# A decoder step on one core: where sixteen groups of cached values stand between the matmuls of the last head

## The chip, the cores and the metric

The kernel runs on one core of a Trainium2 chip. Its time is the device time of one execution in microseconds (us), as the median of several. Five engines work side by side, each through its own list of instructions in order: TensorE (PE, matmuls), VectorE (DVE), ScalarE (ACT), GpSimd (POOL) and SyncE (SP, which here only issues DMAs). They wait for one another through semaphores.

## The reference, cut to what matters

One step of a one-layer decoder: a retention branch of 4 heads and an attention branch of 8 heads ("FoX") are merged and followed by a gated convolution network. Beside a prompt of 1024 tokens there are 8 samples, each with one new token and 4096 cached rows of keys and values, in 32 pages of 128 rows that a page table picks:

```python
k_past = cache_k[l][page_table].reshape(bs, past, FOX_HEADS, FOX_HD)
v_past = cache_v[l][page_table].reshape(bs, past, FOX_HEADS, FOX_HD)
...
# fox_sample
s = jnp.concatenate([jnp.einsum('bqhd,bkhd->bhqk', q, k_past), jnp.einsum('bqhd,bkhd->bhqk', q, k)], axis=-1) * scale
p = jax.nn.softmax(logits, axis=-1)          # logits: s + bias, masked
return (jnp.einsum('bhqk,bkhd->bqhd', p[..., :p_len], v_past)
        + jnp.einsum('bhqk,bkhd->bqhd', p[..., p_len:], v))
```

The change concerns the first of the two products in the last line, for the seventh sample.

## The kernel before, in words

The kernel has four stages; the third one, `retain`, computes the retention branch head by head and does the cached attention of the 8 samples between the matmuls of the heads: two samples for each of the four heads. In head h, PE multiplies the cached values of sample 2h ("values a") and DVE computes the key scores of sample 2h+1 ("keys a") at the same time; after that PE does the values of sample 2h+1 ("values b"), and DVE the keys of the next sample ("keys b", not in the last head).

**Groups.** A sample's 32 pages are 16 groups of two pages (GRP, NG). One group of values is 16 small matmuls on PE (line 948, two pages x four column blocks, each in two passes), all added up in bank 7, which no other matmul of the head uses. One group of keys is a multiply and a reduction on DVE (lines 1245 and 1249, two DVE instructions on 128x1024 elements).

**Loads.** SP issues all loads of keys and values in one list: key group, value group, key group, value group, and so on, two DMAs of 256 KB for each (line 836). Keys and values have rings of 4 buffers each (SLOTS). Before it issues value group i, SP waits until PE has done group i-4 (semaphore `v_used`), and before key group i until DVE has reduced group i-4 (`k_used`). SP runs in a loop of four pairs and reads eight pages' numbers of keys and of values at the head of each round (line 828). While value groups of the seventh sample (sample index 6) are loaded, the keys beside them are those of the eighth.

**Places.** How many groups stand at each place of PE's list is set by a tuple of 22 numbers, VALUES_A_LAST for the last head; KEYS_A_LAST does it for DVE. The sum must be 16. The first six numbers are the places after each of the three chunks of the products w4 and w5 (the retention values, `product`, 24 matmuls a chunk). The next nine are the places in the transpose loop (`rows_t`, lines 1016 and 1018), where parts of the product w6 stand between. The last seven are the places in the retention loop: for each of 8 blocks of 128 tokens PE computes scores and a state update (lines 1043 and 1044), then nine matmuls of w7 (line 142), then, with `out(t-1)`, the block's output before (lines 1032 and 1034), and then the groups. `out(t)` waits for `inner_t` of block t, which DVE makes (line 1362). After block 6, `cache_tail` (lines 955 and 959) closes the sum of the seventh sample.

**DVE's list around it.** DVE does the key groups of the transpose loop, then splits the weights w8 (line 108, `split_lo`, after ACT's `split_hi`, line 101), and only then makes `inner_t` of block 0.

**POOL's list around it.** After ACT has written the last row of the transpose loop (`rows_out`), POOL stores eight rows (line 917) and loads the weights w9, 512 KB (line 93, `load(h, 9)`). The weights w6, w7 and w8 were loaded before.

Of the kernel before, what the change touches and what calls it, by code (L numbers as in the profile page):

```python
# [705 lines left out]
PARTS = NCH * KD  # L706
VALUES_A = (0, 0, 1, 1, 1, 1) + (0, 1, 0, 1, 0, 1, 0, 1, 0) + (1, 0, 1, 1, 0, 1, 1) + (1, 0, 1, 1)
KEYS_A = (1, 1, 1, 1, 1, 1) + (0, 1, 0, 1, 0, 1, 0, 1, 0) + (1, 0, 1, 0, 1, 0, 1) + (2,)
VALUES_A_LAST = (0, 1, 2, 2, 2, 1) + (0, 1, 1, 0, 1, 1, 0, 1, 1) + (1, 0, 1, 0, 0, 0, 0)
KEYS_A_LAST = (1, 2, 1, 1, 2, 1) + (0, 1, 1, 0, 1, 1, 0, 1, 1) + (1, 0, 1, 0, 0, 0, 0)  # L710


# [3 lines left out]
KEYS_B = (4, 2) + (1, 1, 1) + (5,) + (1, 1, 0)  # L716
assert all(sum(s) == NG for s in (VALUES_A, KEYS_A, VALUES_A_LAST, KEYS_A_LAST, VALUES_B, VALUES_B_LAST, KEYS_B))


def take(counts, e):  # L720

    return range(sum(counts[:e]), sum(counts[:e + 1]))
# [7 lines left out]
def retain(nc, g, a, c, o):  # L730
# [4 lines left out]
    with ExitStack() as ctx:  # L735
# [202 lines left out]
        def on_tensor(pe):  # L938
            def cache_values(n, u, i, first):

                slot = i % SLOTS
                if first:
                    pe.wait_ge(prob, n + 1)
                    pe.wait_ge(fos_out, n)
                pe.wait_ge(v_land[slot], n * (NG // SLOTS * GRP * 16) + (i // SLOTS + 1) * GRP * 16)
                for p in range(GRP):
                    for j in range(4):
                        mm = pe.matmul(bank[7][32 * j:32 * j + 2, 0:P], score[u][:, i * GRP + p, 2 * j:2 * j + 2],  # L948
                                       vals[slot][:, p, j * P:(j + 1) * P], start=(first and p == 0), stop=False)
                mm.then_inc(v_used, 1)  # L950
# [22 lines left out]
            def body(h, last):  # L973
                def values_a(e):
                    for i in take(VALUES_A_LAST if last else VALUES_A, e):
                        cache_values(h * 2, 0, i, i == 0)
# [1242 lines left out]
```

## Time and profile before

| | |
|---|---|
| time, median of 3 runs | 2079.36 us (2076.39 to 2080.16) |
| the profiled execution | 2078.71 us, of it span 2076.8 us |
| PE busy | 1964.2 us (95% of the span) |
| DVE busy | 1143.8 us (55%) |
| ACT, POOL busy | 646.4 us (31%), 195.4 us (9%) |
| share of PE in the chain that ended last | 74% |
| mean granted clock of PE | 0.981 |

The last head runs from about 889 to 1016 us of the span. The granted clock is a share of TensorE's full speed of 2.4 GHz; 0.5 is its lower level, 1.2 GHz. A row of the timeline gives the start, the duration, the engine, the line, the operation, its output and inputs, the number of merged instructions, and in brackets the idle time ahead of it with what ended it.

### The profile page before, as it was taken

What the parts mean: (1) busy time and instruction counts of PE and PEld (TensorE: products, weight loads), DVE (VectorE), ACT (ScalarE), POOL (GpSimd) and SP (SyncE); (2) the same over time, 40 slices, a digit from 0 to 9 for tenths busy, and PEclk for the clock granted to TensorE, in tenths of its full rate; (3) what the DMA queues carried; (4) which work ended last, traced back from release to release, by engine and by line L of the source; (5) the groups of instructions that cost most, each with busy time, mean ns of one, the idle gap of its engine ahead of it and who ended that gap; (6) DMA issues with size and microseconds to landing.
All of it is one profiled execution on the core that took longest, in us unless ns stands there. A gap on an engine that the chain in (4) does not pass through costs nothing.

```text
span 2076.8 us, 38216 instructions
## 1 busy us (share of the span) xinstructions
PE 1964.2 (95%) x14259; PEld 1839.1 (89%) x14259; DVE 1143.8 (55%) x1748; ACT 646.4 (31%) x1196; POOL 195.4 (9%) x230
## 2 busy tenths in 40 slices
PE   7999999899999999979899998999999999999996
PEld 5888888788898898868799997999999999999996
DVE  5545646968867866875423857633322333234348
ACT  5445433134134133313401304433202231133334
POOL 1000000111020020010000100000000001000005
PEclk9999999999999999999999999999999999999999
DMA  5111113697987988886833411111111111211154
GB/s 155 43 42 42 41 54 104 216 323 238 323 278 245 314 273 285 285 296 226 283 92 97 119 51 31 32 51 41 51 50 41 51 40 45 58 41 41 38 163 135
DMA packets 151730, 276.63 MB, mean 133 GB/s; under 512 B 19057, under 2 KB 57982, under 8 KB 151590
## 3 DMA queue, kind: packets, MB, share of 16 engines
q1 hardware_dynamic: 115954, 175.22, 25.4%
q0 software_dynamic: 23296, 82.96, 13.7%
q10 hardware_dynamic: 12368, 16.88, 2.2%
q8 instruction: 79, 1.29, 0.3%
q14 instruction: 33, 0.27, 0.0%
HBM read 247.37 MB, written 27.72 MB: 132 GB/s over the span
## 4 chain that ended last, share of the span: by engine, by line
PE 74%; DVE 12%; DMA 4%; issue 4%; SPq 3%; ACT 2%; POOL 0%; ACTq 0%; DVEq 0%; POOLq 0%
PE bank L125 55%; PE bank L142 5%; PE bank L1718 3%; PE bank L521 2%; PE bank L948 2%; DVE cache_keys L1245 2%; PE bank L533 2%; DVE score L1249 2%; SPq L836 2%; DMA cache_keys<-in_cache_k_dram 1%; SPq L828 1%; DMA cache_vals<-in_cache_v_dram 1%; PE banks L505 1%; PE banks L507 1%; DVE w_lo L108 1%
## 5 line engine op out<-in xcount | busy, mean ns | idle before, releaser
L125 PE MATMUL bank<-x_hi,w_hi 128*128 128x344 f32 x1872 | 612.0, 327 | 16.1 <-DVE rot_sin L1315 12.6
L125 PE MATMUL bank<-x_hi,w_lo 128*128 128x344 f32 x1872 | 602.8, 322 | 0.0
L125 PE MATMUL bank<-x_lo,w_hi 128*128 128x344 f32 x1872 | 602.5, 322 | 0.0
L125 PEld LDWEIGHTS bank<-x_hi,w_hi 128*128 128x128 f32 x1872 | 356.3, 190 | 30.0 <-issue 17.4
L125 PEld LDWEIGHTS bank<-x_hi,w_lo 128*128 128x128 f32 x1872 | 356.3, 190 | 0.0
L125 PEld LDWEIGHTS bank<-x_lo,w_hi 128*128 128x128 f32 x1872 | 355.9, 190 | 0.2 <-issue 0.2
L101 ACT ACTIVATE w_hi<-w_raw 128x1024 fp32r<-128x1024 f32 (+3 forms) x139 | 142.1, 1023 | 388.9 <-PE bank L125 371.3
L125 PE MATMUL bank<-moving_lo,w_hi 128*128 128x344 f32 x744 | 239.0, 321 | 0.0
L125 PE MATMUL bank<-moving_hi,w_hi 128*128 128x344 f32 x744 | 226.0, 325 | 9.2 <-DVE moving_lo L1886 3.3
L108 DVE TENSOR_TENSOR w_lo<-w_raw,w_hi 128x1024 fp32r<-128x1024 f32 (+1 forms) x138 | 164.2, 1190 | 87.4 <-ACT w_hi L101 86.8
L125 PE MATMUL bank<-moving_hi,w_lo 128*128 128x344 f32 x648 | 209.0, 323 | 0.0
L1245 DVE TENSOR_TENSOR cache_keys<-cache_keys,q_wide 128x1024 f32<-128x1024 f32 x128 | 156.3, 1223 | 52.3 <-DMA cache_keys<-in_cache_k_dram 52.1
L1249 DVE TENSOR_REDUCE score<-cache_keys 128x16 f32<-128x1024 f32 x128 | 155.1, 1213 | 0.0
L125 PEld LDWEIGHTS bank<-moving_hi,w_hi 128*128 128x128 f32 x744 | 138.6, 191 | 12.7 <-DVE moving_lo L1886 4.6
L125 PEld LDWEIGHTS bank<-moving_lo,w_hi 128*128 128x128 f32 x744 | 141.1, 190 | 0.1
L142 PE MATMUL bank<-x_hi,w_hi 128*128 128x344 f32 x384 | 138.0, 359 | 2.3 <-DVE rv_rows L1419 2.3
L2017 DVE SCALAR_TENSOR_TENSOR stage<-stage,conv_cols_tile 128x1024 f32<-128x1024 f32 x22 | 28.3, 1284 | 185.7 <-ACT stage L1820 185.7
L125 PEld LDWEIGHTS bank<-moving_hi,w_lo 128*128 128x128 f32 x648 | 123.5, 191 | 0.0
L142 PE MATMUL bank<-x_hi,w_lo 128*128 128x344 f32 x384 | 123.0, 320 | 0.0
L142 PE MATMUL bank<-x_lo,w_hi 128*128 128x344 f32 x384 | 122.6, 319 | 0.0
L948 PE MATMUL bank<-cache_vals,score 128*2 128x128 f32 x2048 | 77.8, 274 | 24.0 <-DMA cache_vals<-in_cache_v_dram 19.8
L93 POOL DMA_DIRECT2D w_raw<-in_w_in_dram x53 | 49.0, 925 | 533.6 <-DVE w_lo L108 468.5
(292 smaller groups left out, 2817.8 us busy)
## 6 DMA issues: line engine op xcount, KB each, us to landing
cache_keys<-in_cache_k_dram SPq DMA_DIRECT2D x256, 256.0 KB, 4.9
cache_vals<-in_cache_v_dram SPq DMA_DIRECT2D x256, 256.0 KB, 5.3
w_raw<-in_w_in_dram POOLq DMA_DIRECT2D x52, 512.0 KB, 6.4
w_raw<-in_w_up_dram POOLq DMA_DIRECT2D x22, 512.0 KB, 4.6
w_raw<-in_w_gate_dram POOLq DMA_DIRECT2D x22, 512.0 KB, 4.6
tail_raw<-in_w_down_dram SPq DMA_DIRECT2D x22, 448.0 KB, 3.6
gate<-gate_t_scratch SPq DMA_DIRECT2D x15, 516.0 KB, 3.5
w_raw<-in_w_down_dram POOLq DMA_DIRECT2D x10, 448.0 KB, 4.4
```

The costliest lines, as they stand in the source:

```text
L93: eng.dma_start(g.w_raw[slot][:, 0:kt, 0:m], src).then_inc(g.w_land[slot], 16)
L101: act.activation(g.w_hi[slot][:, 0:kt, 0:m], g.w_raw[slot][:, 0:kt, 0:m], ACT.Copy).then_inc(g.w_rounded, 1)
L108: dve.tensor_tensor(g.w_lo[slot][:, 0:kt, 0:m], g.w_raw[slot][:, 0:kt, 0:m], g.w_hi[slot][:, 0:kt, 0:m].bitcast(F32), ALU.subtract).then_i ...
L125: mm = pe.matmul(g.bank[n][0:m, 0:TC], w[slot][:, k, 0:m], x[:, k, chunk(n)], start=(k == 0 and i == 0), stop=(k == kt - 1 and i == 2))
L142: mm = pe.matmul(g.bank[n][0:m, 0:TC], w[slot][:, k, 0:m], x[:, k, chunk(n)], start=(k == 0 and q == 0), stop=(k == kt - 1 and q == 2))
L521: mm = pe.transpose(bank[part][:, n * P:(n + 1) * P], prob[s % 2][:, blk * P:(blk + 1) * P], g.ident[:])
L533: pe.matmul(b[own(r), 0:P], kv[u][:, blk, 1, own(r)], prob_t[(2 * i + r) % 4][:, blk, :], start=(blk == 0), stop=(blk == i))
L836: sp.dma_start(ring[slot][:, p, :], page).then_inc(land[slot], 16)
L948: mm = pe.matmul(bank[7][32 * j:32 * j + 2, 0:P], score[u][:, i * GRP + p, 2 * j:2 * j + 2], vals[slot][:, p, j * P:(j + 1) * P], start=(f ...
L1245: dve.tensor_tensor(keys[slot][:], keys[slot][:], qb[u][:].unsqueeze(1).to_broadcast([P, GRP, FH * HD]), ALU.mult).then_inc(k_mult, 1)
L1249: dve.tensor_reduce(score[u][:, (i - 1) * GRP:i * GRP, :], keys[slot][:].rearrange("p g (h e) -> p g h e", e=HD), AX.X, ALU.add).then_inc( ...
L1718: mm = pe.matmul(bank[i % NCH][:, 0:hi - lo], w[slot][:, k, :], x[:, k, lo:hi], start=(k == 0 and q == 0), stop=(k == KT - 1 and q == 2))
```

## The change

The tuple of the last head is changed at seven places. The first stage of six places holds 0, 1, 1, 1, 1, 1 groups (five) where it held 0, 1, 2, 2, 2, 1 (eight). The second stage, of nine places, has the same numbers and six groups, but they are the groups 5 to 10 where they were 8 to 13. The third stage holds 1, 1, 1, 1, 1, 0, 0 (five) where it held 1, 0, 1, 0, 0, 0, 0 (two).

```diff
-VALUES_A_LAST = (0, 1, 2, 2, 2, 1) + (0, 1, 1, 0, 1, 1, 0, 1, 1) + (1, 0, 1, 0, 0, 0, 0)
+VALUES_A_LAST = (0, 1, 1, 1, 1, 1) + (0, 1, 1, 0, 1, 1, 0, 1, 1) + (1, 1, 1, 1, 1, 0, 0)
```

The lists of DVE, ACT, POOL and SP are unchanged, and no matmul is added or dropped on PE. The numbers behind `cache_vals` below are the ring's buffers; a group is one row of eight matmuls here (each is two passes in the trace).

PE, in product w5 of the last head, between its first chunk (bank 0) and its second (bank 1), before:

```order
L125 MATMUL bank0<-x_hi,w_hi1 128x344
L125 MATMUL bank0<-x_lo,w_hi1 128x344
L125 MATMUL bank0<-x_hi,w_lo1 128x344
L948 MATMUL bank7<-cache_vals3,score0 2x128 x8
L948 MATMUL bank7<-cache_vals0,score0 2x128 x8
L125 MATMUL bank1<-x_hi,w_hi1 128x344
```

The same place now:

```order
L125 MATMUL bank0<-x_lo,w_hi1 128x344
L125 MATMUL bank0<-x_hi,w_lo1 128x344
L948 MATMUL bank7<-cache_vals2,score0 2x128 x8
L125 MATMUL bank1<-x_hi,w_hi1 128x344
L125 MATMUL bank1<-x_lo,w_hi1 128x344
L125 MATMUL bank1<-x_hi,w_lo1 128x344
```

Two groups (3 and 4) stood here, and now one (group 2): the first reuse of a buffer, `cache_vals0`, has moved to a later place.

PE, in the retention loop, from the last w7 matmuls ahead of `out(0)` to those of block 2, before:

```order
L142 MATMUL bank1<-x_lo,w_hi1 128x344
L142 MATMUL bank1<-x_hi,w_lo1 128x344
L1032 MATMUL banks34<-rv_rows,inner_t 128x256
L1043 MATMUL banks34<-rq_t,rk_t 128x128
L1044 MATMUL banks34<-rv_rows,rk_rows 128x256
L142 MATMUL bank1<-x_hi,w_hi1 128x344
```

The same place now:

```order
L142 MATMUL bank1<-x_lo,w_hi1 128x344
L142 MATMUL bank1<-x_hi,w_lo1 128x344
L1032 MATMUL banks34<-rv_rows,inner_t 128x256
L948 MATMUL bank7<-cache_vals0,score0 2x128 x8
L1043 MATMUL banks34<-rq_t,rk_t 128x128
L1044 MATMUL banks34<-rv_rows,rk_rows 128x256
L142 MATMUL bank1<-x_hi,w_hi1 128x344
```

Group 12 (in buffer 0) now stands behind `out(0)`; before, it stood in the transpose loop. Groups 13, 14 and 15 follow behind `out(1)`, `out(2)` and `out(3)`.

## Rows read from the trace of the kernel before

**Rows 1.** The page: the chain that ended last, shares of the span by engine.

```profile
PE 74%; DVE 12%; DMA 4%; issue 4%; SPq 3%; ACT 2%; POOL 0%; ACTq 0%; DVEq 0%; POOLq 0%
```

**Rows 2.** Waits, 898 to 978 us: who waited for whom, total, times, longest.

```profile
DVE cache_keys L1245 <- DMA cache_keys<-in_cache_k_dram: 11.7, 9, 2.7
...
PE bank L948 <- DMA cache_vals<-in_cache_v_dram: 6.7, 4, 2.6
```

**Rows 3.** Timeline of PE: value groups up to the transpose loop's end.

```profile
902.09 0.62 PE L948 MATMUL bank<-cache_vals,score 128*2 128x128 f32 x16 [3.12 <-issue]
...
908.14 1.05 PE L948 MATMUL bank<-cache_vals,score 128*2 128x128 f32 x32
...
913.10 0.62 PE L948 MATMUL bank<-cache_vals,score 128*2 128x128 f32 x16
914.75 0.62 PE L948 MATMUL bank<-cache_vals,score 128*2 128x128 f32 x16 [1.04 <-DMA cache_vals<-in_cache_v_dram]
...
920.92 0.62 PE L948 MATMUL bank<-cache_vals,score 128*2 128x128 f32 x16 [1.03 <-DMA cache_vals<-in_cache_v_dram]
...
931.88 0.62 PE L948 MATMUL bank<-cache_vals,score 128*2 128x128 f32 x16 [2.62 <-DMA cache_vals<-in_cache_v_dram]
...
946.69 0.62 PE L948 MATMUL bank<-cache_vals,score 128*2 128x128 f32 x16 [2.02 <-DMA cache_vals<-in_cache_v_dram]
```

**Rows 4.** Timeline of PE: retention loop, its first block, `out(0)` and the tail.

```profile
952.63 0.38 PE L1043 MATMUL banks<-rq_t,rk_t 128*128 128x128 f32 x2
...
957.52 0.59 PE L1032 MATMUL banks<-rv_rows,inner_t 128*128 128x256 f32 x2
...
973.45 0.40 PE L955 MATMUL bank<-v_new,score 8*2 8x128 f32 x8
```

**Rows 5.** Timeline of PE: the same place one head earlier.

```profile
777.08 0.42 PE L142 MATMUL bank<-x_hi,w_hi 128*128 128x344 f32 x1
...
780.23 0.38 PE L1043 MATMUL banks<-rq_t,rk_t 128*128 128x128 f32 x2
```

**Rows 6.** Timeline of SP: value group 7, key groups 8 and 13.

```profile
917.60 0.85 SPq L836 DMA_DIRECT2D cache_vals<-in_cache_v_dram  x2
924.57 0.86 SPq L836 DMA_DIRECT2D cache_keys<-in_cache_k_dram  x2
...
942.13 0.85 SPq L836 DMA_DIRECT2D cache_keys<-in_cache_k_dram  x2
```

**Rows 7.** Timeline of DVE: key group 13, weights w8, `inner_t` of block 0.

```profile
948.14 1.23 DVE L1245 TENSOR_TENSOR cache_keys<-cache_keys,q_wide 128x1024 f32<-128x1024 f32 x1 [2.36 <-DMA cache_keys<-in_cache_k_dram]
949.29 1.21 DVE L1249 TENSOR_REDUCE score<-cache_keys 128x16 f32<-128x1024 f32 x1
952.33 1.22 DVE L108 TENSOR_TENSOR w_lo<-w_raw,w_hi 128x1024 fp32r<-128x1024 f32 x1 [1.83 <-ACT w_hi L101]
953.59 0.29 DVE L1362 TENSOR_TENSOR inner_t<-banks,head_const 128x128 f32<-128x128 f32 x1
```

**Rows 8.** Timeline of POOL: store of eight rows, load of the weights w9.

```profile
951.01 0.59 POOL L917 DMA_DIRECT2D own_values_scratch<-rv_rows  x1 [30.65 <-ACT rv_rows L1170]
952.00 0.93 POOL L93 DMA_DIRECT2D w_raw<-in_w_in_dram  x1 [0.40 <-issue]
```

**Rows 9.** Stretches: busy us of each engine; granted clock, DMA share, GB/s stand last.

```profile
889.00:895.00 6.00, 6.00 (x38) 5.95 (x34) 5.85 (x11) 0.00 (x0) 0.00 (x0) 0.64 0.68 230
...
902.00:908.00 6.00, 5.91 (x40) 5.63 (x40) 5.98 (x6) 0.00 (x0) 1.76 (x2) 0.72 1.03 302
...
948.00:952.00 4.00, 4.00 (x29) 2.85 (x29) 2.36 (x2) 1.48 (x3) 0.59 (x2) 0.58 1.04 381
```

**Rows 10.** Timeline of PE: waits ahead of the first stretch of rows 9.

```profile
884.80 0.62 PE L948 MATMUL bank<-cache_vals,score 128*2 128x128 f32 x16 [2.18 <-DMA cache_vals<-in_cache_v_dram]
887.48 1.03 PE L948 MATMUL bank<-cache_vals,score 128*2 128x128 f32 x16 [2.06 <-DMA cache_vals<-in_cache_v_dram]
```

**Rows 11.** The tile of keys, whole kernel: DMA from issue to landing.

```profile
DMA to landing us min/median/max: 2.6/4.9/10.1
```

## The prediction

> **What bounds the kernel now.** I read the page first: the chain that ended last is PE for 74% of it [rows 1]. So whatever PE waits for in the last head is time, as long as nothing else becomes later. Then I read the waits of the stretch in which the values of the seventh sample are multiplied. PE waited 6.7 us in four waits for value groups to land; beside it DVE waited 11.7 us for key groups [rows 2]. The timeline of PE shows which four: 1.04 us at group 4, 1.03 us at group 6, 2.62 us at group 8 and 2.02 us at group 12 [rows 3]. A fifth wait, 3.12 us at group 0, names no DMA [rows 3]; by the code it is for DVE's copy of the sixth sample's output, and group 0 stays at its place, so it stays too. The last thing to read is the other engines at these places, since they decide how much of 6.7 us can come back: SP [rows 6], DVE [rows 7], POOL [rows 8], and the granted clock [rows 9].
>
> **What PE's list gives by itself.** I follow PE from 908.14 us, with every delta against the profiled execution.
> - After the third chunk of w4 there is one group less. Two groups in a row took 908.14 to 909.13 us, a group alone takes about 0.55 us (a row of 0.62 us whose end overlaps the next start), so 0.44 us goes.
> - After the first chunk of w5: groups 3 and 4 began at 913.10 us, and group 4 at 914.75 us behind its wait of 1.04 us [rows 3]. Now group 2 alone stands there: 1.65 us goes, in sum 2.09.
> - After the second chunk the same with groups 5 and 6 and 1.03 us: 1.65 us, in sum 3.74.
> - In the transpose loop the waits of 2.62 and 2.02 us stood ahead of groups 8 and 12. These places now hold groups 5 and 9. Group 5 was used in the first stage before, without any wait of its own, and group 9 is issued right behind group 8 in SP's list, while PE asks for it only at the place of group 12; the four waits of rows 2 are all there were, so group 9 was landed when PE asked for it before. In sum 8.38.
> - The granted clock fell to 0.58 in 948 to 952 us, right behind the 2.02 us wait [rows 9]. From 947.24 us (the end of group 12) to the retention loop at 952.63 us [rows 4] PE took 5.39 us for the rest of w6 and w7, two transposes and one group. One head earlier the same stretch without the group took 777.08 to 780.23 us, 3.15 us [rows 5], and with a group 3.70 us. The low clock cost 1.69 us there. Without the wait it goes: in sum 10.07.
>
> So PE would come to the retention loop at 942.56 us instead of 952.63, and to `out(0)` at 957.52 - 10.07 = 947.45 us [rows 4]. In the loop it has three groups more before the tail (13, 14, 15 and 12 where it had only 15, besides the one at the first place): 3 x 0.55 = 1.65 us. If nothing else were late, the gain would be 10.07 - 1.65 = 8.4 us.
>
> **What is late next.** `out(0)` needs `inner_t` of block 0. DVE makes it behind key group 13 and the weights w8, in that order. Key group 13 is issued at 942.13 us [rows 6] and DVE, which had waited 2.36 us for it, started on it at 948.14 us [rows 7]. This time hangs on SP, not on PE: SP issued the last two rounds of loads back to back, and its last waits in the stretch were before 917.60 us. The change moves that point a little: value group 7 needs value group 3 used, which was at 913.7 us and is now at the fifth place, 919.27 - 2.09 = 917.2 us plus 0.62 us. I put the issue of value group 7 at 918.0 instead of 917.60 us, and since the reading of page numbers (918.45 to 924.57 us [rows 6]) and the issues follow without a gap, everything behind is 0.4 us later: key group 13 at 948.54 us.
> From there DVE needs the multiply (1.15), the reduction (to 950.50 before), the split of w8 (1.26) and `inner_t` (0.29). The 1.83 us that it waited for ACT's half of w8 [rows 7] go, since ACT follows PE, which is 10 us earlier. `inner_t` ends at 953.88 - 1.83 + 0.4 = 952.45 us. PE, at `out(0)` from 947.45 us on, stands for 5.0 us: one wait in place of four. `out(0)` starts 957.52 - 952.5 = 5.0 us earlier than before, and with the three groups the tail comes 5.0 - 1.65 = 3.35 us earlier. Behind that point I find no second bound: blocks 1 to 3 want `inner_t` 2.5 us or more apart, and with one key group each DVE makes them as fast; the groups of the eighth sample stand behind the tail, and the four buffers of the ring are free by 965 us.
>
> **What comes off the 3.35 us.** Two things, neither shown by the trace at this place.
> - The clock. Behind a stand of PE it falls: mean granted 0.58 over 4 us behind 2.02 us of idle, 0.72 over 6 us behind 3.12 us, 0.64 over 6 us behind 2.18 and 2.06 us [rows 3, 9, 10]. Lost are 0.42 x 4 = 1.7, 0.28 x 6 = 1.7 and 0.36 x 6 = 2.2 us. But 2.62 us at 931.88 lost nothing. A stand of 5 us costs between 0 and 2.2 us here; I take 1.5, since part of the low stretch may lie in the stand itself.
> - The load of w9. POOL issues it 1.9 us after the last row of the transpose loop, at 952.00 us [rows 8]. That row comes 9 to 10 us earlier now, so 512 KB more stand in the middle of the last round of key and value loads, where the DMA engines have a share of 1.03 to 1.04 already [rows 9]. At 381 GB/s they take 1.4 us. Key group 13 is then up to 1.4 us later, and so is `inner_t`. Bounds 0 and 1.4 us; I take half, 0.7.
> The Trainium skill, DMA: Bandwidth & Descriptors, "Issuing engines are not separate DMA queues", says that transfers of all issuing engines run on the same 16 DMA engines and interleave. By that rule the w9 load comes off in full (1.4 us) rather than by half; no row here shows such a load among key group 13's packets.
> Sum: 3.35 - 1.5 - 0.7 = 1.15 us faster. The ends are 3.35 (nothing comes off) and 3.35 - 2.2 - 1.4 = -0.25. Against the profiled execution's own 2078.71 us this gives 2077.6. That execution was 0.65 us below the median of the three runs, 2079.36; I forecast 2078.0 us, between.
>
> **The rivals.**
> - *No stand at `out(0)`.* Key group 13 would have to land before PE needs it, about 5 us earlier. Then the whole 8.4 us comes back: 2078.71 - 8.4 = 2070.3. Against it: SP issues without gaps and DVE had waited for this group before. For it only that DMA landings vary.
> - *The stand, but at full clock and without the collision.* 3.35 us faster: 2075.4. For it: 2.62 us of idle at 931.88 left the clock at 1.00.
> - *The keys come much later (slower).* The landing of a key group took 6.0 us for group 13 and up to 10.1 us elsewhere [rows 7, 11]. If w9 and the value groups push group 13 to such a landing, 4.1 us, and the clock costs 2.2, the sum is 3.35 - 4.1 - 2.2 = -2.95: 2081.7. It turns slower once group 13 lands more than about 1.9 us late at 1.5 us of clock. Against it: such landings are rare, the median is 4.9 [rows 11].
> - *The clock as the whole story.* The Trainium skill, TensorE: Matmul & The Clock Gate, "HAM oscillation — how this bites in real kernels", says that a DMA wait of PE that is long enough makes the matmuls behind it start at half clock; one long stand is then worse than several short ones. The trace agrees in part: two of the four short waits had no loss. Worked out from rows as a mechanism of this kernel, it is the stand of 5 to 6.4 us with two losses of the size of rows 9, 1.7 + 1.7, and the collision: 3.35 - 1.4 - 3.4 = -1.45, 2080.2.
>
> **Chances.** The forecast (a stand, a gain between -0.25 and 2.5 us) 0.58; full clock and no collision 0.14; no stand 0.09; two clock losses 0.09; keys much later 0.10. About 0.2%, 4.2 us, is what a measurement of this kernel tells from no change. Faster by more than that: the case without a stand, 0.09, and 0.05 for the good case with a median that falls low, so 0.14. Slower by more: half of the slower rival and a little of the clock's, 0.07. The rest, 0.79, is no change. The range that leaves out the case without a stand and the worst of the slower one is 2074.0 to 2081.5.
>
> **What would show it.** In the trace after: no wait of L948 for values at the first three chunk places, in the transpose loop none or under 1 us; L1043 of block 0 near 942.6 us; a new wait of PE at L1032 for `inner_t`, near 5 us; key group 13 on DVE at 948.5 to 950 us; w9 issued near 942.5 us; the tail L955 at 970 to 973.5 us; a low clock somewhere in 950 to 958 us. Wrong would be: value waits that stay in the transpose loop, a key group 13 that lands before 945 or after 951 us, or a difference that arises behind 979 us.

## The result and the profile after

The changed kernel takes 2081.47 us (median of 20 runs) where the kernel before takes 2077.64 us (20 runs): a ratio of 1.0021, 95% interval 1.0011 to 1.0031 (the two medians alone give 1.0018). It is slower, by 2.3 to 6.4 us; the forecast was 1.2 us faster, 2078.0 us. The measured time lies at the very end of the stated range of 2074.0 to 2081.5 us. A later series gave 1.0017 (1.0004 to 1.0030). The profiled execution has a span of 2083.6 us, 6.8 us more than before, but 2.0 us of that are there already at value group 0 of the last head, ahead of the first changed instruction, and 2.7 us arise behind the tail of the eighth sample. The prediction had called a difference behind 979 us a sign of being wrong, but these two parts can't be put down to the change: a second execution of the changed kernel (e7 below) is 6.3 us shorter ahead of value group 0 and 3.7 us shorter behind the eighth sample, and differs by less than 0.1 us in between. So I count places from the start of value group 0 of the seventh sample, which all kernels have at the same place in PE's list.

The page's chain by engine of the changed kernel, which answers to [rows 1]:

```profile
PE 75%; DVE 11%; DMA 5%; issue 4%; SPq 3%; ACT 2%; POOL 0%; ACTq 0%; DVEq 0%; POOLq 0%
```

PE and DMA have a point more, DVE a point less. The waits from 900 to 982 us answer to [rows 2]:

```profile
DVE cache_keys L1245 <- DMA cache_keys<-in_cache_k_dram: 15.9, 10, 4.7
...
PE banks L1032 <- DVE inner_t L1362: 6.7, 1, 6.7
PE bank L948 <- issue: 3.4, 1, 3.4
```

The four waits for values are gone. In their place is one of the same length, of `out(0)` for `inner_t`. The timeline of PE in the changed kernel, for [rows 3] and [rows 4]:

```profile
904.12 0.62 PE L948 MATMUL bank<-cache_vals,score 128*2 128x128 f32 x16 [3.45 <-issue]
...
944.42 0.38 PE L1043 MATMUL banks<-rq_t,rk_t 128*128 128x128 f32 x2
...
956.17 1.22 PE L1032 MATMUL banks<-rv_rows,inner_t 128*128 128x256 f32 x2 [6.69 <-DVE inner_t L1362]
...
977.41 0.40 PE L955 MATMUL bank<-v_new,score 8*2 8x128 f32 x8
```

Counted from group 0, the loop begins at 40.3 us (50.5 before), `out(0)` at 52.1 (55.4), and the tail comes at 73.3 (71.4). Of the gain of 10.2 us at the loop's start 3.4 us are left at `out(0)`, and at the tail the changed kernel is 1.9 us behind. DVE, SP and POOL, for [rows 7], [rows 6] and [rows 8]:

```profile
952.31 1.23 DVE L1245 TENSOR_TENSOR cache_keys<-cache_keys,q_wide 128x1024 f32<-128x1024 f32 x1 [2.69 <-DMA cache_keys<-in_cache_k_dram]
953.45 1.21 DVE L1249 TENSOR_REDUCE score<-cache_keys 128x16 f32<-128x1024 f32 x1
954.58 1.22 DVE L108 TENSOR_TENSOR w_lo<-w_raw,w_hi 128x1024 fp32r<-128x1024 f32 x1
955.83 0.29 DVE L1362 TENSOR_TENSOR inner_t<-banks,head_const 128x128 f32<-128x128 f32 x1
```

```profile
919.99 0.85 SPq L836 DMA_DIRECT2D cache_vals<-in_cache_v_dram  x2
926.95 0.86 SPq L836 DMA_DIRECT2D cache_keys<-in_cache_k_dram  x2
...
944.49 2.03 SPq L836 DMA_DIRECT2D cache_keys<-in_cache_k_dram  x2
```

```profile
943.40 0.59 POOL L917 DMA_DIRECT2D own_values_scratch<-rv_rows  x1 [19.80 <-ACT rv_rows L1170]
944.39 0.93 POOL L93 DMA_DIRECT2D w_raw<-in_w_in_dram  x1 [0.40 <-issue]
```

DVE does the four steps without a gap from key group 13 on, so `out(0)` is as late as that load. And the w9 load is issued in the same 0.1 us as key group 13. The clock, for [rows 9]:

```profile
952.00:956.00 4.00, 0.00 (x0) 0.00 (x0) 3.66 (x4) 0.00 (x0) 0.00 (x0) 0.55 1.06 393
956.00:960.00 4.00, 3.83 (x23) 2.45 (x24) 3.32 (x7) 0.78 (x2) 0.00 (x0) 0.50 0.48 146
960.00:964.00 4.00, 4.00 (x30) 3.36 (x29) 2.92 (x4) 0.46 (x2) 0.00 (x0) 0.67 0.30 112
```

It stands at the lower level, 1.2 GHz, for nearly all of the last 4 us of the stand (mean 0.55) and for six more behind it. The chain of waits around `out(0)` says the same in one view, the start, the length, and what the time went to:

```profile
944.49 1.51 SPq L836
946.19 6.09 DMA cache_keys<-in_cache_k_dram
952.37 1.08 issue
953.45 1.21 DVE score L1249
954.66 1.13 DVE w_lo L108
956.17 1.22 PE banks L1032 x2
```

In the kernel before, the chain at this place ran from SP over a load of values straight to PE:

```profile
939.93 0.34 SPq L836
941.55 5.10 DMA cache_vals<-in_cache_v_dram
946.69 0.62 PE bank L948 x16
```

### The profile page after: what moved, and what is told of

The parts are those of the page before. It is cut to its first block, busy times and chain, and to the rows that moved or that the text cites. A ratio compares the mean times of both kernels' runs of the same rounds, so it can differ in the third digit from the quotient of the medians.

```text
span 2083.6 us, 38216 instructions
## 1 busy us (share of the span) xinstructions
PE 1973.0 (95%) x14259; PEld 1844.5 (89%) x14259; DVE 1143.4 (55%) x1748; ACT 646.8 (31%) x1196; POOL 195.4 (9%) x230
## 4 chain that ended last, share of the span: by engine, by line
PE 75%; DVE 11%; DMA 5%; issue 4%; SPq 3%; ACT 2%; POOL 0%; ACTq 0%; DVEq 0%; POOLq 0%
PE bank L125 55%; PE bank L142 5%; PE bank L1718 3%; PE bank L948 2%; PE bank L521 2%; PE bank L533 2%; DMA cache_keys<-in_cache_k_dram 2%; DVE score L1249 2%; DVE cache_keys L1245 1%; SPq L836 1%; DMA cache_vals<-in_cache_v_dram 1%; SPq L828 1%; PE banks L505 1%; PE banks L507 1%; DVE w_lo L108 1%
```

## The experiments

Theory K: the change lets PE run ahead until it meets `inner_t` of block 0, which hangs on the load of key group 13; the clock that falls behind this one stand, and dearer places of the groups, turn the gain into a loss. Rival G: the loss is the price of the groups in the retention loop. Rival M: keys only move a wait. All ratios are to the kernel before on the same chip, with 95% intervals, from 12 runs each (e5: 6, the first series of the changed kernel: 20). The times are in us, of the one profiled execution of each, counted from value group 0.

| kernel | loop starts | out(0) | tail | ratio |
|---|---|---|---|---|
| before | 50.5 | 55.4 | 71.4 | 1 |
| changed | 40.3 | 52.1 | 73.3 | 1.0021 (1.0011 to 1.0031) |
| changed again, e7 | 40.3 | 52.1 | 73.3 | 1.0017 (1.0004 to 1.0030) |
| w9 late, e1 | 41.6 | 52.9 | 73.2 | 1.0009 (0.9993 to 1.0025) |
| w9 late again, e11 | 38.8 | 50.0 | 70.1 | 0.9999 (0.9985 to 1.0013) |
| filler, e6 | 41.5 | 53.4 | 73.3 | 1.0004 (0.9995 to 1.0014) |
| seven, six, three, e4 | 49.5 | 55.2 | 71.9 | 0.9995 (0.9982 to 1.0007) |
| before, keys behind, e3 | 48.8 | 53.7 | 71.1 | 1.0015 (0.9998 to 1.0032) |
| key group 13 behind, e8 | 40.3 | 48.2 | 68.0 | 0.9984 (0.9969 to 0.9998) |
| keys 12, 13 behind, e2 | 40.3 | 45.2 | 64.1 | 0.9975 (0.9958 to 0.9992) |
| the same again, e9 | 41.2 | 46.1 | 65.0 | 0.9975 (0.9961 to 0.9989) |
| keys behind, w9 late, e5 | 40.3 | 45.2 | 63.8 | 0.9951 (0.9935 to 0.9968) |
| the same again, e10 | 38.8 | 43.7 | 62.0 | 0.9961 (0.9944 to 0.9977) |

**Key groups behind `inner_t` (e2, again e9).** On the changed kernel:

```diff
-KEYS_A_LAST = (1, 2, 1, 1, 2, 1) + (0, 1, 1, 0, 1, 1, 0, 1, 1) + (1, 0, 1, 0, 0, 0, 0)
+KEYS_A_LAST = (1, 2, 1, 1, 2, 1) + (0, 1, 1, 0, 1, 1, 0, 0, 0) + (1, 1, 1, 1, 0, 0, 0)
```

> The changed kernel, with DVE's key groups 12 and 13 moved behind inner_t of block 0 (keys of the last head 1,2,1,1,2,1 / 0,1,1,0,1,1,0,0,0 / 1,1,1,1,0,0,0). Theory K: inner_t of block 0 no longer waits for a key load, PE's wait of 6.7 us ahead of out(0) and the 3.1 us of low clock behind it go, value group 12 may wait 0 to 1.5 us: 7 to 9.5 us faster than the changed kernel, ratio to before 0.9975 to 0.9990. Rival G: the wait is only cover, and the groups keep their price: ratio stays above 1.001. Rival M (the keys only move the wait: DVE comes late at inner_t of blocks 1 to 3 instead): waits of the same 5 to 7 us in total at later L1032, ratio 1.001 to 1.003.

> The kernel of e2 once more (key groups 12 and 13 behind inner_t, w9 early), beside e10 on the same chip: ratio 0.9965 to 0.9980; value group 12 waits 0.4 to 1 us; the tail 64 us behind value group 0.

Both came as theory K has it. The timeline of PE in e2:

```profile
946.13 0.59 PE L1032 MATMUL banks<-rv_rows,inner_t 128*128 128x256 f32 x2
...
947.37 0.62 PE L948 MATMUL bank<-cache_vals,score 128*2 128x128 f32 x16 [0.65 <-DMA cache_vals<-in_cache_v_dram]
```

and of DVE:

```profile
941.55 1.23 DVE L108 TENSOR_TENSOR w_lo<-w_raw,w_hi 128x1024 fp32r<-128x1024 f32 x1 [1.16 <-ACT w_hi L101]
942.81 0.29 DVE L1362 TENSOR_TENSOR inner_t<-banks,head_const 128x128 f32<-128x128 f32 x1
943.92 1.23 DVE L1245 TENSOR_TENSOR cache_keys<-cache_keys,q_wide 128x1024 f32<-128x1024 f32 x1 [0.49 <-DMA cache_keys<-in_cache_k_dram]
```

There is no wait at L1032 and none for later `inner_t`, so rival M falls. `out(0)` and the tail come 6.8 and 9.2 us earlier than in the changed kernel, which is the stand of 6.7 us and the 3.0 us of low clock behind it, less the new wait of 0.65 us. The ratios, 0.9975 and 1.0021, are some 9.6 us apart, about the same. Rival G falls as the whole story: the values stand as in the changed kernel. In e9 a wait of 0.60 us was at value group 13, the next one, and not at 12.

**One key group (e8).** Only group 13 moved: the second stage of the keys is (0, 1, 1, 0, 1, 1, 0, 1, 0) and the third (1, 1, 1, 0, 0, 0, 0).

> The changed kernel with only key group 13 moved behind inner_t of block 0. Theory K: inner_t then follows key group 12, which reaches DVE about 43 us behind value group 0: plus 1.15 + 1.13 + 1.26 + 0.29 gives 46.9, so out(0) stands 1 to 2 us in place of 6.7 and the clock holds: 6 to 8 us faster than the changed kernel, about 1 us behind e2, ratio 0.9975 to 0.9990. Rival: if not group 13 but DVE's load in general were late, the stand would shrink by one group's 2.3 us only, ratio about 1.001.

```profile
953.13 1.22 PE L1032 MATMUL banks<-rv_rows,inner_t 128*128 128x256 f32 x2 [2.86 <-DVE inner_t L1362]
```

The stand went from 6.7 to 2.9 us and the tail came 5.3 us earlier: more than a group's 2.3 us of DVE work, so it is the load of group 13 and not DVE's work. The stand is longer than expected (2.9 for 1 to 2), since group 12 came at 44.4 us, and the clock still fell, at a cost of 1.5 us.

**The same key order on the kernel before (e3).**

> The kernel before, with the same move of key groups 12 and 13 behind inner_t of block 0. Theory K: PE did not wait for inner_t there, its waits are for values, so the move alone gives nothing: ratio 0.9995 to 1.0005, value waits still 6 to 7 us. If the key order by itself is worth the time, 0.997 to 0.999.

```profile
932.68 0.62 PE L948 MATMUL bank<-cache_vals,score 128*2 128x128 f32 x16 [2.34 <-DMA cache_vals<-in_cache_v_dram]
...
947.38 0.62 PE L948 MATMUL bank<-cache_vals,score 128*2 128x128 f32 x16 [1.90 <-DMA cache_vals<-in_cache_v_dram]
963.13 0.62 PE L948 MATMUL bank<-cache_vals,score 128*2 128x128 f32 x16 [1.37 <-DMA cache_vals<-in_cache_v_dram]
```

The value waits stay and there is one more, 7.8 us in all where 6 to 7 were expected. No gain: the ratio's middle is above the range expected, its interval holds 1. So moving the keys gained nothing here, where PE still waits for values; it gained in the changed kernel, where PE arrives early.

**Half of the change (e4).** Values `(0, 1, 1, 2, 2, 1) + (0, 1, 1, 0, 1, 1, 0, 1, 1) + (1, 0, 1, 1, 0, 0, 0)`.

> Half of the change: value groups seven, six and three over the stages (0,1,1,2,2,1 / 0,1,1,0,1,1,0,1,1 / 1,0,1,1,0,0,0). Theory K: out(0) starts when DVE's inner_t is there, as in the changed kernel, however PE's list ahead of it looks; the stand is split, 3 to 5 us at value group 12 ahead of the loop and 1 to 3 us at L1032, and with two groups fewer in the retention loop the kernel is 1 to 2 us faster than the changed one, ratio to before 1.0008 to 1.0016. Rival G (price of the groups in the loop alone, 0.75 us each beyond 0.5): ratio 1.0005 or less, with the value waits gone.

```profile
941.42 1.03 PE L948 MATMUL bank<-cache_vals,score 128*2 128x128 f32 x16 [4.09 <-DMA cache_vals<-in_cache_v_dram]
...
950.85 0.59 PE L1032 MATMUL banks<-rv_rows,inner_t 128*128 128x256 f32 x2
```

The wait at value group 12 is there, the one at L1032 is not: my expectation was wrong in this. Group 12's load, and the low clock behind it, hold PE until DVE is ready and longer: `inner_t` is there at 51.6 us, PE comes at 55.2. So two loads of the same round of SP close the way, group 12 of the values and group 13 of the keys; only one of them is moved by the change. The time is no different from before. The ratio is below the 1.0008 to 1.0016 that I expected of theory K; the trace's tail, 71.9 us, is 1.4 us ahead of the changed kernel's, as was expected.

**The w9 load (e1, again e11).** On the changed kernel, in POOL's body for the last head:

```diff
+                if last:
+                    wait_apart(pool, o_mm, h * NB + 1, g.mm_chunk)
                 load(h, 9)
```

> The changed kernel, but POOL issues the load of the weights w9 only after out(0) of the last head. Theory K (the time is set by DVE's inner_t of block 0, which stands behind key group 13, and the w9 load delays that group): key group 13 reaches DVE 1 to 2 us earlier than in the changed kernel, counted from group 0 of the values (there 952.31 - 904.12 = 48.2 us; expected 46.2 to 47.2), the wait of PE ahead of L1032 shrinks from 6.7 us to 5 to 5.7, and the kernel is 1.4 to 2.5 us faster than the changed one: ratio to before 1.0009 to 1.0014. Rival G (the loss is the price of value groups in the retention loop, not a wait): nothing changes, 1.0021.

> The kernel of e1 once more (changed, w9 late). In e1's trace the low clock behind value group 0 came 1.3 us later for PE, and with it SP's issue of value group 7. If that was the reason why key group 13 reached DVE at 49.0 us behind group 0, then in an execution whose retention loop begins at 40.3 us, as in the changed kernel, key group 13 should be at 46.5 to 47.5 us; if it is at 48 us or later there too, the w9 load does not delay it.

PE in e1, then in e11:

```profile
902.37 1.03 PE L950 MATMUL bank<-cache_vals,score 128*2 128x128 f32 x16 [2.87 <-issue]
...
955.22 1.22 PE L1034 MATMUL banks<-rv_rows,inner_t 128*128 128x256 f32 x2 [6.21 <-DVE inner_t L1364]
```

```profile
901.51 0.62 PE L950 MATMUL bank<-cache_vals,score 128*2 128x128 f32 x16 [2.13 <-issue]
```

(Lines behind 917 stand two higher here.) In e1 key group 13 reached DVE at 49.0 us, not at 46.2 to 47.2, and the stand was 6.2 us. What hid the effect in e1 was the clock. Behind the stand at group 0, which lies ahead of all that was changed, PE came to group 1 after 4.5 us in e11, 6.0 in the changed kernel and 7.3 in e1, where all the matmuls between are the same; the loop began at 38.8, 40.3 and 41.6 us. SP follows: since value group 7 waits for group 3, its round, and with it key group 13, moves with PE (46.1, 48.2 and 49.0 us). So I count from the loop's start: group 13 comes 7.4 and 7.3 us behind it with w9 late, and 7.9 and 8.0 us in the two executions of the changed kernel. By this count the w9 load costs 0.6 us of the stand. Counted from SP's issue of key group 13 it is more: 6.8 and 6.6 us from issue to DVE with w9 late, 7.8 and 7.8 in the changed kernel. The two counts differ since SP reached this issue at another distance from the loop's start in e1 and e11. So the price for `inner_t` is between 0.6 and 1.1 us, where I had expected 1 to 2. DVE in e11 shows what stays:

```profile
944.95 1.23 DVE L1247 TENSOR_TENSOR cache_keys<-cache_keys,q_wide 128x1024 f32<-128x1024 f32 x1 [5.57 <-DMA cache_keys<-in_cache_k_dram]
947.63 1.23 DVE L1247 TENSOR_TENSOR cache_keys<-cache_keys,q_wide 128x1024 f32<-128x1024 f32 x1 [0.33 <-DMA cache_keys<-in_cache_k_dram]
```

Here group 12 is the late one and group 13 follows it at DVE's own pace; why group 12's load took longer than in the changed kernel, 6.2 us from issue for 5.0, no run tells. (It took 6.3 us in e1, 5.8 in e8, which has w9 early.) No changed kernel with w9 late began its loop at 40.3 us; e11's began 1.5 us earlier, and moved by that its key group 13 would be at 47.6 us, just outside the 46.5 to 47.5 expected. By the series, w9 late gave 1.0009 and 0.9999 where the changed kernel gave 1.0021 and 1.0017, but the intervals overlap, so they don't show a gain of w9 late by itself.

**Filler (e6).** Ahead of `out(0)` in the last head, on the changed kernel:

```diff
+                    if last and t == 1:
+                        pe.wait_ge(g.bank_free[2], first(h) + 8)
+                        for k in range(28):
+                            pe.matmul(g.bank[2][0:P, 0:TC], g.w_hi[head_job(h, 7)[1]][:, k % KD, 0:P], g.xh[:, k % KD, chunk(2)],
+                                      start=True, stop=True)
```

> The changed kernel with 28 spare matmuls of 344 columns in the last head, ahead of out(0), where PE only waits; their result is written over by w7's third chunk. Theory C (some 3 us of the loss is the low clock behind the stand): the spare matmuls take 28 x 0.157 = 4.4 us of the stand of 6.7 us, PE still waits 1 to 3 us at L1032, the clock stays at 1.00 behind it, and from out(0) to L1034 it takes 3 us instead of 6.7: 2.5 to 3.1 us faster than the changed kernel. If the clock were not the cause of the slow stretch behind out(0), nothing is gained, or the 28 matmuls cost time.

```profile
946.78 4.58 PE L1050 MATMUL bank<-x_hi,w_hi 128*128 128x344 f32 x28
953.82 0.88 PE L1032 MATMUL banks<-rv_rows,inner_t 128*128 128x256 f32 x2 [2.46 <-DVE inner_t L1367]
```

From `out(0)` to `out(1)`'s second part (line 1034) it took 5.3 us for 6.7. So spare work in the stand gives back 1.4 us, half of what was expected: behind the 2.5 us that were left the clock was low again. The tail of this execution is where the changed kernel's is, since its loop began 1.2 us later. The series cannot tell it apart from e7 (1.0004 and 1.0017).

**The changed kernel again (e7).**

> The changed kernel once more, to be compared with e6 and e8 on the same chip: ratio 1.001 to 1.003; in its trace the wait at L1032 is between 5 and 7.5 us.

The wait was 6.77 us, the tail at 73.3 us as in the first execution. So the picture of the trace is not one execution's accident.

**Both (e5, again e10).** e2's keys and e1's w9.

> Key groups 12 and 13 behind inner_t of block 0 as in e2, and the w9 load after out(0) as in e1. If the w9 load delays the groups around it (theory W), value group 12, which waited 0.65 us in e2, waits less or nothing: 0.5 to 1 us faster than e2. If not (which e1 speaks for, where the stand was still 6.2 us), the same as e2 within noise, ratio 0.997 to 0.998, with a wait of 0.3 to 1.5 us.

> The kernel of e5 once more (as e2, with the w9 load after out(0)). By the traces the w9 load is worth 0.3 us (tail 63.8 against 64.1 us), so the ratio should be within 0.0005 of that of e2: 0.9963 to 0.9980. If w9 really is worth the 5 us between the medians of e2 and e5, it stays near 0.995.

This has the lowest medians, 2067.63 (6 runs) and 2069.97 us. Its value waits were 0.36 us and none. From the loop's start to the tail it is 0.3 us (e5 against e2) and 0.6 us (e10 against e9) shorter. By the medians it is 4.7 us ahead (e5 against e2, on different chips) and 2.1 us (e10 against e9, on one chip), but the intervals overlap. So what w9 is worth here is not shown; e10's 0.9961 is just below the 0.9963 to 0.9980 of its first expectation, and not near the 0.995 of the second.

## Why the prediction was wrong

The mechanism was the one forecast: which waits go, the new one, its place and cause. Three sizes behind it were too small, the load of key group 13, the low clock and the groups in the loop, and together they turned the sign. By its steps, against the profiled execution and from group 0:

- *PE's own list.* 10.07 us forecast at the loop's start, 10.2 measured. Right, the 1.69 us of low clock among it.
- *What is late next.* Right in place. `out(0)` was forecast 5.0 - 0.7 = 4.3 us earlier and was 3.4. The SP term held: value group 7 was forecast at 15.9 us and issued at 15.9, key group 13 at 40.4 and issued at 40.4. The missing 0.9 us lie in the load of key group 13: from issue to DVE 6.0 + 0.7 = 6.7 us were forecast, and it took 7.8. I had taken the one landing that I had for the rule. The rows of SP show where 1.2 of the 1.8 us above 6.0 arise: the issue of the pair itself took 2.03 us where it had taken 0.85. In the kernel before, the slow issue of this round was the value pair behind it, where it delayed no key group 13:

```profile
943.22 1.54 SPq L836 DMA_DIRECT2D cache_vals<-in_cache_v_dram  x2
```

  In e1 and e11, with w9 late, the issue of key group 13 was slow too, 1.7 and 1.5 us, and in e8 again the pair behind it. So of the 1.8 us the w9 load made 0.6 to 1.1, where I had put 0.7, and the rest goes with the slow issue having fallen on this pair; what makes it slow, and how much of it is w9, is open. The Trainium skill, DMA: Bandwidth & Descriptors, "Issuing engines are not separate DMA queues", says that DMAs of all issuing engines run on the same 16 DMA engines and interleave. The trace agrees: w9 (issued at 944.39 us, 7.0 us to its landing) and key group 13 were under way together. The full price of 1.4 us, which the prediction drew from this, was not seen.
- *The clock: the term that failed most.* I took 1.5 us. From `out(0)` to the tail the changed kernel took 21.2 us, and e10, which has the same matmuls and no wait, 18.3 us: 3.0 us of low clock (e7: 2.9). I had priced a stand of 5 us by rows of 2 to 4 us, and then took less than they showed, for the part that lies in the stand. The stretch at the lower level did not end when PE began again: 6 us of work ran in it. The prediction also says that two of the four short waits had no loss. It was three: the granted clock was 1.00 behind those of 1.04, 1.03 and 2.62 us. So what the change gave up was one loss of 1.7 us, and what it got was one of 3.0.
- *Groups in the loop.* 1.65 us forecast for three. Before, `out(0)` to the tail was 15.9 us; in e10, without waits, it is 18.3 with three more: 2.3 us, 0.77 each. A group alone between product matmuls cost 0.55; between `out(t)` and the scores' matmuls it costs 0.2 more. The two timelines of blocks show it. Changed:

```profile
966.16 0.59 PE L1032 MATMUL banks<-rv_rows,inner_t 128*128 128x256 f32 x2
...
967.12 0.62 PE L948 MATMUL bank<-cache_vals,score 128*2 128x128 f32 x16
...
969.86 0.59 PE L1032 MATMUL banks<-rv_rows,inner_t 128*128 128x256 f32 x2
```

Before, a block without a group:

```profile
966.63 0.59 PE L1032 MATMUL banks<-rv_rows,inner_t 128*128 128x256 f32 x2
...
969.56 0.59 PE L1032 MATMUL banks<-rv_rows,inner_t 128*128 128x256 f32 x2
```

3.70 against 2.93 us.

In sum -3.4 + 3.0 + 2.3 = +1.9 us at the tail, where -1.15 was forecast. Of the rivals, the one with two clock losses was nearest: it gave 1.45 us slower where the tail came 1.9 us later, though the loss came as one stretch of 3.0 us and not as two of 1.7. Its chance of 0.09 was too low: the stand was the central part of the forecast, and in the rows the longest one, 3.12 us, had a loss, as had the two of 2.18 and 2.06 us in a row.

What stays open: the series say 3.8 us slower by the medians (2.3 to 6.4 by the interval; in the later series the medians are 2.2 us apart), the traces 1.9, the same in both executions. The lower end nearly meets. A part may be that the changed kernel passes on what the kernel before swallowed. Its value waits made the tail come at 71.4 and 71.1 us (before and e3) though the low clock behind group 0 took 1.5 us in one and nothing in the other, while in the changed orders the loop's start and key group 13 moved with it. That is argued from few executions and not shown.

## What to carry to other kernels

When waits for one stream of loads are taken away, look for the next wait on the same issuing engine's list: here both streams are issued by one engine in one order, and moving the consumer of one stream only made PE meet the other. Move both consumers together (values and keys: 0.9975, and 0.9961 and 0.9951 with the weights' load out of the way), or neither. And several short waits merged into one long one are not the same wait: add the low clock behind the long one, and don't price it by the shorter ones (here 3.0 us lost behind 6.7, where the rows of 2 to 4 us showed 0 to 2.2).

## What had not been expected of the hardware

- Behind the stand of 6.7 us TensorE ran at the lower level for 6 us of work, 3.0 us lost, though it had begun at once with dense matmuls; behind 2.9 us in e8 1.5 us were lost; behind 4.1 us at one value group in e4 the granted clock was 0.50 from 940 to 944 us and 0.65 from 944 to 948.
- The loss behind one and the same stand differs from execution to execution: behind a stand of 3.5 us at group 0 PE took 6.0 us for the same 24 matmuls and the group in the changed kernel, e2, e5, e7 and e8, and 7.0 and 7.2 us in e9 and e6. Behind 2.9 us in e1 it took 7.3 us, behind 2.0 to 2.1 us in e3, e10 and e11 4.5 us, and behind 2.2 us in e4 6.0 us.
- In the last round of loads one of SP's first four issues of two DMAs took 1.3 to 2.1 us in every execution, where the others take 0.85 to 1.2; which one it is changes. What SP waits for there is not shown.
- A small group of 16 matmuls costs 0.44 us behind another group, 0.55 alone between the matmuls of 344 columns and 0.77 between the shorter ones of the retention loop.
